# The second layer's norm taken in two halves, with the projection's blocks in another order

## The chip, the cores and the metric

One NeuronCore of one Trainium2 chip runs the whole program. The metric is the device time of one execution in microseconds; three runs of the kernel before gave 2537.19 to 2538.4, with a median of 2538.09.

## What is computed

Two blocks of a model follow one another. The change touches only the first, a two-layer block over 256 tokens of x and 256 tokens of context, model width 1024. Each layer norms its input, shifts and scales it by terms that differ for x and for the context, mixes, and adds the result. The second layer (the "odd" one) needs from its projection this:

```python
xl = rms_norm(h_lat, norm_w[li]) * (1.0 + scale_l[:, None, :]) + shift_l[:, None, :]
xc = rms_norm(h_ctx, norm_w[li]) * (1.0 + scale_c) + shift_c
cq_l, ckv_l, kr_l, z_l = jnp.split(xl @ w_in, ODD_SPLITS, axis=-1)   # 256, 128, 64, 1024 columns
cq_c, ckv_c, kr_c, z_c = jnp.split(xc @ w_in, ODD_SPLITS, axis=-1)
qn_l, qr_l = queries(cq_l, seq)          # rms_norm(cq, q_norm_w) @ wq_b
k_l, v_l = keys_values(ckv_l, kr_l_rot, seq)
k_c, v_c = keys_values(ckv_c, kr_c, clen)
out_l = (o_l.reshape(bsz, seq, C_WIDTH) * jax.nn.silu(z_l)) @ w_out
```

The query latent cq and the gate z are used for x alone. Only the key/value latent ckv (with its rotary part) is used for the context too.

## The kernel before

Every engine has its own program in each stage (an `nc.Block()`), and a stage starts when all engines have ended the one before it. Activations stand feature-major: the residual `k.h` is 128 partitions x 8 chunks x 512 tokens, tokens 0 to 255 of x and 256 to 511 of the context. A float32 product is made of three: operand and weight are split into a high and a low part (`xn_hi`/`xn_lo`, `w_hi`/`w_lo`), and hi*hi, hi*lo and lo*hi are summed in a PSUM bank.

Weights come in blocks of up to 256 columns through a ring of four slots, in the order of `k.plan`, filled by SyncE; a slot is free when its `w_lo` is made. `Split` cuts a block into four parts (`PARTS`), each two of the eight chunks deep. ScalarE copies a part to `w_hi` (L366), and GpSimd subtracts to get `w_lo` (L375); there are four buffers of each, so ScalarE waits for TensorE to have used the part four back (`consumed`).

The stages around the change:

- `project_out(..., "even")` ends the first layer. Beside it `EarlySquares` squares the new residual on ScalarE (L923), adds up six of the chunks' squares on VectorE, and TensorE, at its end, sums the rest over partitions with a matrix of ones into bank 7 (L910, L913), 512 tokens at a time.
- `odd_project` is the stage in question. `project` runs it: TensorE first does `norm.hum` warming products (`hum`, L270) that have no result, then blocks 0 to 5: cq (256 columns, 2 token groups of x), ckv (192 columns, 4 token groups, x and context), and four z blocks (256 columns, feature-major, x alone). Before each part of block 0 it waits for the two chunks of `xn` that the part needs.
- `RmsNorm` makes `xn` in it. VectorE scales the sum (`ask_root`, L255), ScalarE takes the root (L265, `root`), VectorE the reciprocal (L258), all 512 tokens wide. Then a pipeline goes over the eight chunks: VectorE `h * rstd` (L803), ScalarE shift and scale (L835, once for x and once for the context) and copy to `xn_hi` (L840), VectorE subtraction to `xn_lo` (L856).
- The program of ScalarE, VectorE and GpSimd in `project` is one loop over b from -1: first the `w_hi` and `w_lo` of block b+1, then (at b = -1) the norm, then the copies of block b out of its PSUM banks, then what `LatentNorms` has for this b. Each engine takes its instructions in this order.
- `LatentNorms` norms the latents. VectorE takes squares and sums (L1491, L1493), asks for the root (L1522, L1524), applies the rotary terms (L1060 to L1065, L1532), and scales (L1538). TensorE turns the latents (L1504, L1507) before block 4, and VectorE copies them out (L1544, L1546).
- `odd_queries` is the next stage; its first products (L1596) read the turned latents.

## Time and profile before

| | us |
|---|---|
| median of three runs | 2538.09 (2537.19 to 2538.4) |
| the profiled execution | 2540.84 |
| its span in the trace | 2539.1 |
| TensorE busy, of the span | 2404.1 |
| VectorE busy | 1640.1 |
| ScalarE busy | 1310.7 |
| GpSimd busy | 597.5 |

The stretch that the change touches is some 65 us near 360 to 423 of the span. All times in the rows are from the span's start. In a timeline a row "start, length" may merge several instructions of one form ("x4"); the brackets at its end tell how long its engine stood idle before it and which instruction ended that. Instructions of one engine overlap a little, so a row's start can lie before the end of the one above.

### The profile page before, as it was taken

The page shows a single profiled execution, that of the slowest core. Times are in us where ns is not written, and L with a number is a line of the kernel's source. Part 1 is how long each engine was busy: PE and PEld are TensorE (multiplying, and loading weights), DVE is VectorE, ACT ScalarE, POOL GpSimd, SP SyncE. Part 2 cuts the span into 40 slices and gives each one's busy share as a digit, 9 for nine tenths or more (in the row PEclk, how much of TensorE's full clock was granted, in tenths as well). Part 3 has the DMA queues.
Part 4 walks back from the last instruction along what each step waited for, and adds up shares of the span by engine and source line. Part 5 has one row for each costly group of instructions (what it writes and reads, how often), then busy time and mean ns, then how long its engine had stood idle before and what let it go on. Part 6 is the DMA issues. An engine that isn't in the chain of part 4 may idle for free. (4 is left out here: it accounts for less than half of the span.)

```text
span 2539.1 us, 61096 instructions
## 1 busy us (share of the span) xinstructions
PE 2404.1 (95%) x22840; PEld 2268.0 (89%) x22840; DVE 1640.1 (65%) x3412; ACT 1310.7 (52%) x2403; POOL 597.5 (24%) x484
## 2 busy tenths in 40 slices
PE   5999788999989999999999999879999999999998
PEld 3998567578978999999999999768999999999997
DVE  3032643535445967778888666665967778888666
ACT  3322643456346665555445554556666555445554
POOL 0335134158336930000000000636920000000000
PEclk8999999999999999999999999989999999999999
DMA  8554023043123555444444554324555444444552
GB/s 277 160 173 150 17 63 108 28 129 123 44 67 129 190 188 181 164 163 159 166 164 164 189 190 157 126 76 134 188 192 168 164 165 166 166 165 165 185 194 84
DMA packets 153875, 373.31 MB, mean 147 GB/s; under 512 B 8920, under 2 KB 102888, under 8 KB 137232
## 3 DMA queue, kind: packets, MB, share of 16 engines
q1 hardware_dynamic: 151232, 369.27, 43.3%
q10 hardware_dynamic: 2512, 2.24, 0.3%
q8 instruction: 88, 1.44, 0.2%
q14 instruction: 43, 0.35, 0.0%
HBM read 370.44 MB, written 1.05 MB: 146 GB/s over the span
## 5 line engine op out<-in xcount | busy, mean ns | idle before, releaser
L3027 ACT ACTIVATE w_hi<-ring 128x512 fp32r<-128x512 f32 x1024 | 641.8, 632 | 674.0 <-PE bank L3082 360.4
L3033 DVE TENSOR_TENSOR w_lo<-ring,w_hi 128x512 fp32r<-128x512 f32 x864 | 589.2, 690 | 330.5 <-ACT w_hi L3027 323.6
L3082 PE MATMUL bank<-hidden_hi,w_hi 128*128 128x256 f32 x2048 | 574.9, 281 | 1.4 <-ACT hidden_hi L3165 1.4
L3064 PE MATMUL bank<-x_hi,w_hi 128*128 128x256 f32 x2048 | 575.4, 281 | 0.2
L3082 PE MATMUL bank<-hidden_hi,w_lo 128*128 128x256 f32 x2048 | 573.1, 280 | 0.0
L3064 PE MATMUL bank<-x_hi,w_lo 128*128 128x256 f32 x2048 | 572.3, 279 | 0.0
L3064 PE MATMUL bank<-x_lo,w_hi 128*128 128x256 f32 x2048 | 571.0, 279 | 0.0
L3082 PE MATMUL bank<-hidden_lo,w_hi 128*128 128x256 f32 x2048 | 570.2, 278 | 0.0
L375 POOL TENSOR_TENSOR w_lo<-ring,w_hi 128x512 fp32r<-128x512 f32 (+3 forms) x260 | 338.6, 1321 | 663.5 <-ACT w_hi L366 655.0
L3082 PEld LDWEIGHTS bank<-hidden_hi,w_hi 128*128 128x128 f32 x2048 | 385.1, 188 | 1.6 <-issue 1.6
L3064 PEld LDWEIGHTS bank<-x_hi,w_hi 128*128 128x128 f32 x2048 | 385.0, 188 | 0.8 <-ACT w_hi L3027 0.6
L3082 PEld LDWEIGHTS bank<-hidden_lo,w_hi 128*128 128x128 f32 x2048 | 385.1, 188 | 0.0
L3064 PEld LDWEIGHTS bank<-x_lo,w_hi 128*128 128x128 f32 x2048 | 385.1, 188 | 0.0
L3064 PEld LDWEIGHTS bank<-x_hi,w_lo 128*128 128x128 f32 x2048 | 384.8, 188 | 0.0
L3082 PEld LDWEIGHTS bank<-hidden_hi,w_lo 128*128 128x128 f32 x2048 | 384.8, 188 | 0.0
L366 ACT ACTIVATE w_hi<-ring 128x512 fp32r<-128x512 f32 (+2 forms) x264 | 157.2, 614 | 285.2 <-PE bank L465 273.6
L3429 POOL MEMSET small<- 128x128 f32 x2 | 0.4, 207 | 949.6 <-DVE hidden L3324 949.6
L3033 POOL TENSOR_TENSOR w_lo<-ring,w_hi 128x512 fp32r<-128x512 f32 x160 | 203.3, 1301 | 33.5 <-ACT w_hi L3027 30.5
L465 PE MATMUL bank<-w_hi,xn_hi 128*128 128x256 f32 (+1 forms) x496 | 141.9, 286 | 4.5 <-DVE xn_lo L856 4.0
L465 PE MATMUL bank<-w_lo,xn_hi 128*128 128x256 f32 (+1 forms) x496 | 139.7, 282 | 0.0
L465 PE MATMUL bank<-w_hi,xn_lo 128*128 128x256 f32 (+1 forms) x496 | 139.4, 281 | 0.0
L3317 DVE TENSOR_TENSOR small<-small 128x1536 bf16<-128x1536 bf16 x128 | 121.8, 952 | 0.0
(518 smaller groups left out, 3966.5 us busy)
## 6 DMA issues: line engine op xcount, KB each, us to landing
ring<-in_peer_uT SPq DMA_DIRECT2D x128, 1024.0 KB, 4.9
ring<-in_peer_v SPq DMA_DIRECT2D x128, 1024.0 KB, 4.8
ring<-in_even_w_in SPq DMA_DIRECT2D x26, 1024.0 KB, 5.4
ring<-in_ada_w SPq DMA_DIRECT2D x24, 1024.0 KB, 7.8
ring<-in_odd_w_in SPq DMA_DIRECT2D x12, 1024.0 KB, 5.3
ring<-in_even_w_out SPq DMA_DIRECT2D x8, 1024.0 KB, 5.7
ring<-in_odd_w_out SPq DMA_DIRECT2D x8, 1024.0 KB, 5.2
ring<-in_peer_w_q SPq DMA_DIRECT2D x8, 1024.0 KB, 5.1
```

Source lines behind the costliest of these rows:

```text
L366: act.activation(k.hi[g % PARTS][:, 0:n], src, ACT.Copy).then_inc(k.hi_ready, 1)
L375: eng.tensor_tensor(k.lo[g % PARTS][:, 0:n], src, k.hi[g % PARTS][:, 0:n].bitcast(F32), ALU.subtract).then_inc(k.lo_ready, 1)
L465: mm = pe.matmul(out, lhs, rhs, start=(j == 0 and cc == 0 and q == 0), stop=(cc == KC - 1 and q == 2), skip_group_check=True)
L3027: act.activation(k.hi[q][:, :], k.ring[slot][:, q * PART:q * PART + PART], ACT.Copy).then_inc(k.hi_ready, 1)
L3033: eng.tensor_tensor(k.lo[q][:, :], k.ring[slot][:, q * PART:q * PART + PART], k.hi[q][:, :].bitcast(F32), ALU.subtract).then_inc(k.lo_read ...
L3064: mm = pe.matmul(k.bank[s][:, j * T:j * T + T], a[q][:, w], b[:, cc, :], start=(cc == 0 and n == 0), stop=(cc == KC - 1 and n == 2))
L3082: mm = pe.matmul(out, a[q][:, w], b[:, j, :], start=first and cc % 2 == 0 and n == 0, stop=last and cc % 2 == 1 and n == 2, skip_group_che ...
L3317: dve.tensor_tensor(right, spread(hot, 2, 3), spread(self.gateT[:, at, :, :], 3, HALF_J // 2), ALU.mult).then_inc(self.ready, 1)
L3429: pool.memset(self.k.ones, 1.0).then_inc(self.ones_ready, 1)
```

## The change

The norm of the second layer is taken by halves of 256 tokens: `early` is "halves". The sums go to two banks (7 for x, 6 for the context), the root of the first half is asked for and taken first, and on ScalarE it stands ahead of the `w_hi` copies of block 0. The chunk pipeline runs over the eight chunks of x; the second root follows; the pipeline over the context's chunks (`rest`) comes in the loop at b = 0, behind the `w_hi` and `w_lo` of block 1 and the copies of block 0. The blocks come in the order cq, z0, z1, ckv, z2, z3, so that the one that reads the context is the fourth, and the weights are planned in the same order. TensorE waits for the context's chunks at block 3. The steps of `LatentNorms` move along: the sums of cq to b = 1, those of ckv to b = 3, rotary and scaling to b = 4, the transposes behind block 5 and the copies to b = 5. The warming products of this stage are 12 in place of 48.

```diff
@@ project
+                    if norm and norm.halves and b == 3:
+                        norm.wait_chunk(pe, KC + KC // PARTS * (part + 1) - 1)
...
+                if norm and norm.halves and b == 0 and name != "pool":
+                    norm.rest(name, eng)
@@ RmsNorm
-        self.hum = {0: 8, 1: 48, None: 54}[layer]
+        self.hum = {0: 8, 1: 12, None: 54}[layer]
+        self.halves = early == "halves"
+        self.sums = [k.bank[7][:, 0:T], k.bank[6][:, 0:T]]
+    def ask_half(self, dve, half):
+        t = slice(half * T, half * T + T)
+        dve.wait_ge(self.summed, half + 1)
+        self.k.ask_root(dve, self.rstd[:, t], 1.0 / D, 1e-6, self.sums[half])
+    def scalar_half(self, act, half):
+        k = self.k
+        done = []
+        for i in range(KC * half, KC * half + KC + 1):
+            if i < KC * half + KC:
+                c, _, t = self.half_of(i)
+                act.wait_ge(self.scaled, i + 1)
+                o = self.work[:, c, t]
+                done.append(k.act.step(act.activation(o, o, ACT.Identity, bias=k.mod[:, self.layer, c, half:half + 1],
+                                                      scale=k.mod[:, self.layer, 8 + c, half:half + 1])))
+            if i > KC * half:
+                c, _, t = self.half_of(i - 1)
+                k.act.settle(act, done[c])
+                act.activation(self.out[0][:, c, t], self.work[:, c, t], ACT.Copy).then_inc(self.rounded, 1)
+    def vector_half(self, dve, half):
+        for i in range(KC * half, KC * half + KC + 2):
+            if i < KC * half + KC:
+                c, _, t = self.half_of(i)
+                dve.tensor_tensor(self.work[:, c, t], self.k.h[:, c, t], self.rstd[:, t], ALU.mult).then_inc(self.scaled, 1)
+            if i >= KC * half + 2:
+                c, _, t = self.half_of(i - 2)
+                dve.wait_ge(self.rounded, i - 1)
+                dve.tensor_tensor(self.out[1][:, c, t], self.work[:, c, t], self.out[0][:, c, t].bitcast(F32), ALU.subtract).then_inc(self.ready, 1)
+    def rest(self, name, eng):
+        (self.scalar_half if name == "act" else self.vector_half)(eng, 1)
     def squares(self, act):
-        pass
+        if self.halves:
+            self.root_half(act, 0)
     def scalar(self, act):
+        if self.halves:
+            self.scalar_half(act, 0)
+            self.root_half(act, 1)
+            return
     def vector(self, dve):
+        if self.halves:
+            self.ask_half(dve, 0)
+            self.vector_half(dve, 0)
+            self.ask_half(dve, 1)
+            return
@@ EarlySquares.tensor
+        if self.rms.halves:
+            halves = [(self.rms.sums[s], slice(s * T, s * T + T)) for s in range(2)]
+            for out, t in halves:
+                pe.matmul(out, k.ones[:, :], self.acc[:, t], start=True, stop=False)
+            pe.wait_ge(self.squared, KC)
+            for out, t in halves:
+                pe.matmul(out, k.ones[:, :], self.sq[:, 0, t], start=False, stop=False)
+                pe.matmul(out, k.ones[:, :], self.sq[:, 1, t], start=False, stop=True).then_inc(self.rms.summed, 1)
+            return
@@ odd_project
+    at = ["cq", 0, 1, "ckv", 2, 3]
+    width = {"cq": C_Q, "ckv": C_KV + C_R}
...
@@ LatentNorms
     def tensor(self, pe, b):
-        if b != 4:
+        if b != 6:
             return
         k = self.k
         pe.wait_ge(self.normed, 1)
-        pe.wait_ge(k.drained["dve"], self.counts[1]["dve"])
+        pe.wait_ge(k.drained["dve"], self.counts[3]["dve"])
+        pe.wait_ge(k.drained["act"], self.counts[4]["act"])
     def scalar(self, act, b):
-        if b == 2:
+        if b == 4:
             self.k.root(act, self.ss[:, :])
     def vector(self, dve, b):
-        if b == 0:
+        if b == 1:
...
-        if b == 1:
+        if b == 3:
...
+        if b == 4:
             for m in range(4):
...
-        if b == 2:
             dve.wait_ge(k.rooted, k.asked)
...
-        if b == 4:
+        if b == 5:
             dve.wait_ge(self.turned, 1)
@@ plan_weights
-    plan_columns(k, d["odd_w_in"], 0, C_Q)
-    plan_columns(k, d["odd_w_in"], C_Q, C_Q + C_KV + C_R)
-    plan_columns(k, d["odd_w_in"], C_Q + C_KV + C_R, C_Q + C_KV + C_R + D)
+    z = C_Q + C_KV + C_R
+    for c0, c1 in ((0, C_Q), (z, z + 2 * WB), (C_Q, z), (z + 2 * WB, z + D)):
+        plan_columns(k, d["odd_w_in"], c0, c1)
```

## Rows read from the trace of the kernel before

**Rows 1.** The page, busy time of each engine over the span.
```profile
PE 2404.1 (95%) x22840; PEld 2268.0 (89%) x22840; DVE 1640.1 (65%) x3412; ACT 1310.7 (52%) x2403; POOL 597.5 (24%) x484
```

**Rows 2.** Waits of TensorE, 350 to 425: total, times, longest.
```profile
PE bank L1504 <- DVE ckv L1538: 5.4, 1, 5.4
```

**Rows 3.** Timeline of TensorE, 355 to 423: start, length, instruction, idle before.
```profile
355.62 1.98 PE L913 MATMUL bank<-sq_even,ones 128*128 128x512 f32 x4 [1.60 <-ACT sq_even L923]
357.93 10.52 PE L270 MATMUL bank<-ident 128*128 128x512 bf16 x48 [0.32 <-PEq L419]
369.79 0.36 PE L465 MATMUL bank<-w_hi,xn_hi 128*128 128x256 f32 x1 [1.34 <-DVE xn_lo L856]
...
401.30 0.28 PE L465 MATMUL bank<-xn_hi,w_lo 128*128 128x256 f32 x1
407.00 1.08 PE L1504 MATMUL bank<-ident,cq 128*128 128x128 f32 x4 [5.42 <-DVE ckv L1538]
...
409.45 0.56 PE L465 MATMUL bank<-xn_hi,w_hi 128*128 128x256 f32 x1
...
422.93 3.69 PE L1596 MATMUL bank<-cqT,ring 128*128 128x256 f32 x16 [0.94 <-PEq L419]
```

**Rows 4.** Timeline of ScalarE, 354 to 377.
```profile
354.94 1.15 ACT L923 ACTIVATE sq_even<-residual 128x512 f32<-128x512 f32 x2 [10.08 <-DVE residual L1672]
357.96 2.19 ACT L366 ACTIVATE w_hi<-ring 128x512 fp32r<-128x512 f32 x4 [1.87 <-PEq L419]
360.06 0.61 ACT L265 ACTIVATE rms_rstd<-rms_rstd 128x512 f32<-128x512 f32 x1
364.82 2.08 ACT L835 ACTIVATE normed<-normed,mod 128x256 f32<-128x256 f32 x4 [4.15 <-DVE normed L803]
...
376.87 1.33 ACT L366 ACTIVATE w_hi<-ring 128x384 fp32r<-128x384 f32 x3
```

**Rows 5.** Timeline of VectorE, 360 to 412.
```profile
360.70 3.35 DVE L258 RECIPROCAL rms_rstd<-rms_rstd 128x512 f32<-128x512 f32 x1 [2.08 <-ACT rms_rstd L265]
...
379.62 0.76 DVE L520 COPY cq<-bank 128x256 f32<-128x256 f32 x2 [1.85 <-PE bank L465]
...
390.39 1.15 DVE L520 COPY ckv<-bank 128x192 f32<-128x192 f32 x4 [7.93 <-PE bank L465]
...
398.11 0.17 DVE L1524 TENSOR_SCALAR odd_ss<-odd_ss 128x4 f32<-128x4 f32 x1
...
400.79 2.89 DVE L1538 SCALAR_TENSOR_TENSOR cq<-cq,odd_ss,rows 128x256 f32<-128x256 f32 x2
403.60 3.14 DVE L1538 SCALAR_TENSOR_TENSOR ckv<-ckv,odd_ss,rows 128x128 f32<-128x128 f32 x4
...
410.44 1.28 DVE L1546 COPY ckvT<-bank 128x512 f32<-128x512 f32 x2
```

**Rows 6.** Timeline of GpSimd, 358 to 407.
```profile
358.67 4.96 POOL L375 TENSOR_TENSOR w_lo<-ring,w_hi 128x512 fp32r<-128x512 f32 x4 [14.64 <-ACT w_hi L366]
...
400.71 5.36 POOL L375 TENSOR_TENSOR w_lo<-ring,w_hi 128x512 fp32r<-128x512 f32 x4 [2.66 <-ACT w_hi L366]
```

**Rows 7.** Line 1538, the four ckv scalings: min/median/max ns, first and last start.
```profile
L1538 DVE SCALAR_TENSOR_TENSOR ckv<-ckv,odd_ss,rows x4: 338/842/1349, 403.6 to 406.4; 128x128 f32<-128x128 f32 x4
```

**Rows 8.** Timeline of VectorE in the final norm, 256 tokens wide.
```profile
531.81 1.75 DVE L258 RECIPROCAL rms_rstd<-rms_rstd 128x256 f32<-128x256 f32 x1 [2.92 <-ACT rms_rstd L265]
533.60 1.10 DVE L803 TENSOR_TENSOR normed<-residual,rms_rstd 128x256 f32<-128x256 f32 x3
...
540.24 0.76 DVE L856 TENSOR_TENSOR x_lo<-normed,x_hi 128x256 fp32r<-128x256 f32 x2 [0.52 <-ACT x_hi L840]
```

**Rows 9.** Timeline of ScalarE there.
```profile
531.36 0.42 ACT L265 ACTIVATE rms_rstd<-rms_rstd 128x256 f32<-128x256 f32 x1
```

**Rows 10.** Half-microsecond windows: length, busy of each engine, granted clock (PEclk), DMA.
```profile
404.50:405.00 0.50, 0.00 (x0) 0.00 (x0) 0.50 (x2) 0.00 (x0) 0.50 (x2) 0.64 0.00 0
...
411.00:411.50 0.50, 0.50 (x5) 0.50 (x3) 0.50 (x2) 0.00 (x0) 0.00 (x0) 0.53 0.00 0
```

More of the change, by code:

```diff
@@ L785, in sum, with half_of, root_half @@
             mm.then_inc(self.summed, 1)
+    def half_of(self, i):
+        half, c = divmod(i, KC)
+        return c, half, slice(half * T, half * T + T)
+    def ask_half(self, dve, half):
+        t = slice(half * T, half * T + T)
+        dve.wait_ge(self.summed, half + 1)
+        self.k.ask_root(dve, self.rstd[:, t], 1.0 / D, 1e-6, self.sums[half])
+    def root_half(self, act, half):
+        self.k.root(act, self.rstd[:, half * T:half * T + T])
+    def scalar_half(self, act, half):
[23 more added lines that the diff above has]
+        (self.scalar_half if name == "act" else self.vector_half)(eng, 1)
     def shift_chunk(self, act, c):
@@ L1457, in odd_project @@
 def odd_project(k, xn, cq, ckv, zT, norm, beside):
+    at = ["cq", 0, 1, "ckv", 2, 3]
+    width = {"cq": C_Q, "ckv": C_KV + C_R}
     def outs(b):
-        if b < 2:
-            return [("token", m) for m in range(2 if b == 0 else 4)]
+        if at[b] in width:
+            return [("token", m) for m in range(2 if at[b] == "cq" else 4)]
         return [("feature", [(0, P), (P, 2 * P)])]
     def store(name, eng, b, i, bank):
-        if b < 2:
-            dst = cq[:, i, :] if b == 0 else ckv[:, i, 0:C_KV + C_R]
+        if at[b] in width:
+            dst = cq[:, i, :] if at[b] == "cq" else ckv[:, i, 0:C_KV + C_R]
             return copy(name, eng, dst, bank[:, 0:dst.shape[1]])
-        return copy(name, eng, zT[:, 2 * (b - 2):2 * (b - 2) + 2, :], bank[:, :].rearrange("p (f t) -> p f t", f=2), ACT.Silu)
-    project(k, xn, T, [WB, C_KV + C_R] + [WB] * 4, outs, store, lambda b, i: "dve" if b < 2 else "act", norm=norm, beside=beside)
+        return copy(name, eng, zT[:, 2 * at[b]:2 * at[b] + 2, :], bank[:, :].rearrange("p (f t) -> p f t", f=2), ACT.Silu)
+    project(k, xn, T, [width.get(x, WB) for x in at], outs, store, lambda b, i: "dve" if at[b] in width else "act", norm=norm, beside=beside)
 class LatentNorms:
@@ L1515, in vector @@
         k, S = self.k, self.k.dve
-        if b == 0:
+        if b == 1:
             dve.wait_ge(k.drained["dve"], self.counts[0]["dve"])
             self.sums(dve, self.jobs()[0:2], 0)
-        if b == 1:
-            dve.wait_ge(k.drained["dve"], self.counts[1]["dve"])
+        if b == 3:
+            dve.wait_ge(k.drained["dve"], self.counts[3]["dve"])
             self.sums(dve, self.jobs()[2:6], 2)
@@ L1715, in first_block @@
             to_feature_major(k, jobs, "even_mix", True)
-            rms = RmsNorm(k, 1, TC, rstd, "sums")
+            rms = RmsNorm(k, 1, TC, rstd, "halves")
             project_out(k, mixT, TC, residual(0), "even", EarlySquares(k, rms, "even"))
@@ L1778, in __init__ @@
         self.hum = 24
+        self.halves = False
         k.norms += 1
```

## The prediction

> **What bounds the kernel now.** The page's first line comes first: TensorE is busy 2404 of 2539 us, so time is saved only where TensorE stands still or runs at a low clock [rows 1]. The reader then goes to the stretch that the diff touches, the projection of the second layer, from the end of the stage before it to the first product of the stage after it. TensorE's own timeline gives its borders [rows 3]: the sums of squares end at 357.60, the warming products run 357.93 to 368.45, the first product of the projection starts at 369.79, the transposes wait until 407.00, and the next stage starts at 422.93. Two holes stand in it. The first is 357.6 to 369.8, the norm. The second is 5.4 us before the transposes, which the list of waits puts on the scaling of the latents by VectorE [rows 2]. The ScalarE, VectorE and GpSimd timelines then tell what fills these holes [rows 4 to 6], and the granted clock tells what the second costs after it [rows 10]: TensorE stopped at 401.58, the grant fell to half at about 404.6 (3.1 us later), and came back at about 411.5, 4.5 us after work resumed at 407.0. TensorE loses half of such a stretch, about 2.2 us.
>
> **One fact that carries the sum.** While GpSimd has its subtraction w_lo running, a VectorE instruction with two SBUF tensors waits for it. The six latent scalings took 2.89 us for two and 3.14 us for four while GpSimd had four w_lo in a row [rows 5, 6]; one alone, after GpSimd was done, took 0.34 us against up to 1.35 [rows 7]. GpSimd's four took 5.36 us there and 4.96 us when VectorE was doing a one-tensor operation: 1.24 us each alone, and about 1.41 us for a pair of one w_lo and one VectorE operation.
>
> The page "Advanced Engine Details and Errata" of the Trainium skill, section "GPSIMD Details", says the Pool engine shares a read and a write interface with VectorE and conflicts with VectorE instructions of two SBUF inputs. That is the rule under the rows just named, and by it the third rival below could not happen; the rows alone already make it unlikely.
>
> **The change part by part,** on the clock of the trace of before.
>
> (a) The sums. The last two squares end at 356.09 [rows 4]. Now both halves wait for the second square, and eight 256-column records follow at about 0.21 us each, where 512-column ones took 0.43 and the first pair started at 355.62 [rows 3]. They end about 0.5 us later, near 358.1, and the next stage starts near 358.4: a loss of 0.5.
>
> (b) The first root. Its three steps at 256 columns: a scaling of 0.42 (the width of the three that took 1.10 together, starts 0.34 apart [rows 8]), the root 0.42 [rows 9], the reciprocal 1.75 [rows 8]. It now goes ahead of the four w_hi copies (2.19 us [rows 4]). It ends at 358.4 + 2.6 + about 0.1 = 361.1, where before it ended at 360.70 + 3.35 = 364.05 [rows 5].
>
> (c) The collision. Before, GpSimd's four w_lo were done at 363.63, ahead of the first scaling [rows 6]. Now w_hi begins at 359.2, w_lo at 359.9, and these go on to 365.4 beside VectorE's chunks. The first three scalings and the first x_lo each wait for one w_lo: they end at 361.5, 362.9, 364.3 and 365.7. The second x_lo follows at 366.4, and block 0's first product can start at 366.5: 3.3 us before 369.79, not the 5 or more that the halved norm alone would give.
>
> (d) Block 0. The warming is cut to 12 products, 12/48 of 10.52, so it ends at 361.2, and TensorE stands still for 5.3 us. I take it that the grant falls, as it did in the 5.4 us hole. Eight z parts took 390.39 to 401.58, so a part is 1.40 us and a block 5.6. From 366.5 the low level lasts to 371.0, with 2.24 us of full-rate work done. The remaining 3.4 end at 374.4, where before block 0 ended at 379.6 (VectorE starts on it at 379.62 [rows 5]). At full clock it would be bound by the chunks and end near 373. The lead is 5.2 us.
>
> (e) The second half. A first half pass takes 7.40 us from the first scaling to the last x_lo at this width in the final norm (533.60 to 541.00 [rows 8]); here ScalarE's shift costs about 0.50 a piece (four in 2.08 [rows 4]) against about 0.4 there, so I take 7.8. With the collision the first pass ends at 371.2. VectorE's second root takes 2.7, to 373.9, then the two copies of block 0 (0.76 [rows 5]) at 374.4, and only at 375.2 the second pass. Two w_lo of block 1 are still to come, so two scalings wait for them, another 2.0 us, and ScalarE issues its last x_hi copy at 384.5. Queued behind it on ScalarE are the w_hi copies of block 2 (the loop takes them after the norm's rest), and behind these GpSimd's w_lo: 0.63 + 1.3 + slack gives TensorE its block 2 at 386.6. Block 1 runs 374.4 to 380.1. So a new hole of 6.5 us opens between z blocks, where before there was none, and the clock falls in it too: 2.24 us lost after it. This hole is what eats the lead.
>
> (f) The rest of the blocks. Block 2: 386.6 + 5.6 + 2.24 = 394.5. Block 3, the context's, took 379.62 to 390.39: 10.7 to 10.8, so 405.2. Blocks 4 and 5: 11.3, so 416.5.
>
> (g) The latents. From the end of the ckv block to the root's request took 7.9 us (390.39 to 398.28 [rows 5]), with GpSimd's w_lo beside it, and so it will be: 413.2. Rotary terms and reciprocal take 2.5 us more (to 400.79). The six scalings cost 5.95 us before under w_lo; now block 5's last w_lo is over by 413, and they go at their own pace, at 0.26 to 0.34 each and slack: 2.0. So normed is at 417.7 and TensorE waits 1.2 us at the transposes in place of 5.4. At full clock the transposes take half of the 2.45 us between 407.00 and 409.45 [rows 3]. The copies out of PSUM now stand bare, where before block 4 covered them: from the transposes' end at 409.45 to 411.72 [rows 3, 5], 2.2 us. With 0.33 for the border of the stages (357.60 to 357.93) the next stage starts at 417.7 + 1.2 + 2.2 + 0.3 = 421.4, against 422.93. That is a gain of 1.5 to 1.6 us.
>
> (h) Weights. The same six blocks are loaded in another order; a slot comes free when its w_lo is done, so the fifth and sixth blocks are asked for at 365 and 378, over 20 us before use: nothing. The moved root of the latents and its table load on ScalarE stand before VectorE's request and cost nothing. If that cover went, the table load would be 1.3 us.
>
> The same sum by the skill's page "VectorE: DVE Perf Modes", section "The TRN2 errata": it asks for tiles of at least 512 elements, since each instruction pays a fixed part, and gives an fp32 tensor_tensor (N+151)/0.96 ns. By that, an estimate, 32 half-width operations cost 13.6 us where 16 full ones cost 11.0, so 2.6 us against the change. The trace agrees on single durations (0.42 here) but the operations overlap at 0.34 apart, so the sum above goes by these.
>
> **The sum.** -1.6 us. The profiled execution took 2540.84 us around a span of 2539.1, the median of the shown runs is 2538.09; the difference is applied to the median: 2536.5.
>
> **The rivals.**
> - Small holes (0.2). The grant doesn't fall before block 0, or comes back sooner, and the second pass misses one w_lo: up to 1.4 + 1.3 + 1.0 more. Together about 2533.5. For it: 5.3 us is near the length at which the rows show one fall. Against it: block 2 still waits for the whole second pass.
> - The clock at the end (0.2), the slower side. In the last 5 us TensorE works only 1.25 us, between a wait of 1.2 and one of 2.5. If the grant falls there, the transposes cost 1.2 more and the next stage's first 4.5 us lose 2.2; with a later return after the middle hole, 1.2 more. That is -1.6 + 4.6 = +3.0: 2541.1. [...]
> - No collision (0.05). If VectorE and GpSimd didn't exclude each other, block 0 starts at 364.4, block 2 at 381.6, and the next stage at about 415.5: 2531. Against it speak [rows 5 to 7].
> - The change doesn't do what it says (0.05). If block 0 starts no earlier than before, since the w_hi copies and w_lo hold the first half up, the 3.3 us of (c) are lost and the time is about 2539.8.
> - My forecast, with holes of 5 and 6.5 us and a gain of 0 to 3 us: 0.5.
>
> **The numbers.** Measurement can tell about 0.2%, 5.1 us, from no change. Only the third rival and the far end of the first pass that line below (0.08 together), and only the second with a further fall passes it above (0.05). Same: 0.87. The range takes in the first, second and fourth: 2532.5 to 2541.5.
>
> **What would show it.** In the new profile: the first product of block 0 near 366.5; VectorE's first scalings each ending just after a w_lo; a TensorE hole of about 6.5 us between blocks 1 and 2, put on w_hi or w_lo of block 2; the granted clock at 0.5 behind it; a wait of 1 to 2 us before the transposes and short latent scalings. The forecast is wrong if block 2 starts before 383, if the scalings are short while w_lo runs, or if the next stage starts at half clock.

## The result, and the profile after

The changed kernel took 2543.16 us (median of 20 runs) where the kernel before took 2539.11 (20 runs) in the same comparison: a ratio of 1.0016, 95% interval 1.001 to 1.0022. That is slower by about 4 us, outside the forecast range and on its other side. The span of the profiled execution was 2542.0 us.

The page, busy time of each engine: TensorE is busy as long as before [rows 1], so the page by itself says only that the time was lost where TensorE stood still, and not where that was. It executes 30 instructions less; remember the count.

```profile
PE 2403.7 (95%) x22810; PEld 2273.0 (89%) x22810; DVE 1643.6 (65%) x3430; ACT 1312.4 (52%) x2412; POOL 597.0 (23%) x484
```

**The changed stage is faster, as forecast.** TensorE's timeline after, which answers to [rows 3] (start, length, instruction, idle before). This execution reached the stage 1.28 us earlier (the last product of the residual ended at 351.88, before at 353.16):

```profile
357.18 2.75 PE L270 MATMUL bank<-ident 128*128 128x512 bf16 x12 [0.32 <-PEq L419]
365.33 0.55 PE L467 MATMUL bank<-w_hi,xn_hi 128*128 128x256 f32 x1 [5.41 <-DVE xn_lo L828]
...
385.50 0.55 PE L467 MATMUL bank<-xn_hi,w_hi 128*128 128x256 f32 x1 [5.90 <-ACT w_hi L366]
...
416.41 1.04 PE L1576 MATMUL bank<-ident,ckv 128*128 128x128 f32 x8
```

TensorE's waits from 355 to 421 (total, times, longest) answer to [rows 2]. The single wait of 5.4 us for the latents is gone; two of 5.4 and 5.9, one of 1.1 and one of 2.2 have come, and the wait for the last squares has grown from 1.6 [rows 3] to 2.1:

```profile
PE bank L467 <- ACT w_hi L366: 5.9, 1, 5.9
PE bank L467 <- DVE xn_lo L828: 5.4, 1, 5.4
PE bank L1665 <- PEq L419: 2.2, 1, 2.2
PE bank L972 <- ACT sq_even L988: 2.1, 1, 2.1
PE bank L1573 <- DVE ckv L1607: 1.1, 1, 1.1
```

VectorE's timeline, against [rows 5]: the first three scalings of the norm take 3.24 us beside GpSimd's w_lo, while the six latent scalings, now free of it, take 2.0 where they took 6.0.

```profile
359.87 3.24 DVE L824 TENSOR_TENSOR normed<-residual,rms_rstd 128x256 f32<-128x256 f32 x3
...
413.93 0.88 DVE L1607 SCALAR_TENSOR_TENSOR cq<-cq,odd_ss,rows 128x256 f32<-128x256 f32 x2
414.73 1.13 DVE L1607 SCALAR_TENSOR_TENSOR ckv<-ckv,odd_ss,rows 128x128 f32<-128x128 f32 x4
```

The windows below give length, busy time of TensorE, weight loads, VectorE, ScalarE and GpSimd, then granted clock, DMA share and GB/s. TensorE's clock is at its lower level, 1.2 GHz (0.50), behind each of the two long holes, and at 2.4 GHz (1.00) in the rest of the stage.

```profile
364.50:371.50 7.00, 6.17 (x29) 6.20 (x30) 5.45 (x15) 5.70 (x14) 0.06 (x1) 0.51 0.49 150
371.50:381.50 10.00, 8.10 (x69) 7.89 (x67) 7.48 (x15) 6.71 (x15) 5.16 (x4) 1.00 0.35 105
382.00:388.00 6.00, 2.50 (x12) 2.53 (x13) 3.44 (x8) 5.33 (x10) 4.00 (x4) 0.50 0.00 0
```

From the last product of the residual to the next stage's first product the stage takes 67.81 us; before it took 69.77 [rows 3]. So 2.0 us were gained here, and by the medians some 6 lost elsewhere; between the two profiled executions, whose spans differ by 2.9 us, it is 4.9.

**Where they were lost.** ScalarE's table loads are good landmarks: each execution has the same 92, in the same order. From one to the next, the two traces agree within their usual scatter but for one place, 130 us behind the changed stage, in the second block's recurrent projection. First before, then after (ScalarE's timeline):

```profile
550.87 1.28 ACT L1932 ACT_TABLE_LOAD   x1
553.92 1.28 ACT L1933 ACT_TABLE_LOAD   x1
575.86 1.28 ACT L1945 ACT_TABLE_LOAD   x1
```

```profile
547.57 1.28 ACT L2002 ACT_TABLE_LOAD   x1
552.28 1.28 ACT L2003 ACT_TABLE_LOAD   x1
576.82 1.28 ACT L2015 ACT_TABLE_LOAD   x1
```

I call the two stretches A and B. They took 3.05 and 21.94 us before, 4.71 and 24.54 after: 4.3 us lost, in code that the change doesn't touch. VectorE's timeline shows how A grew, first before, then after:

```profile
548.55 0.17 DVE L2003 TENSOR_TENSOR rk_heads<-cpart,cols 128x8 f32<-128x8 f32 x1 [0.28 <-DMA mu_lora<-in_mu_lora]
548.75 0.42 DVE L2007 TENSOR_TENSOR gkoT<-ktT 64x255 f32<-64x255 f32 x1
549.26 1.33 DVE L2009 SCALAR_TENSOR_TENSOR ktT<-gkoT,mu_lora,ktT 64x256 f32<-64x256 f32 x1
```

```profile
545.70 1.18 DVE L2073 TENSOR_TENSOR rk_heads<-cpart,cols 128x8 f32<-128x8 f32 x1 [0.71 <-DMA mu_lora<-in_mu_lora]
```

GpSimd's row of four w_lo in the same stretch, first before, then after (GpSimd's timeline):

```profile
548.84 5.76 POOL L375 TENSOR_TENSOR w_lo<-ring,w_hi 128x512 fp32r<-128x512 f32 x4 [0.84 <-ACT w_hi L366]
```

```profile
545.56 5.39 POOL L375 TENSOR_TENSOR w_lo<-ring,w_hi 128x512 fp32r<-128x512 f32 x4 [0.85 <-ACT w_hi L366]
```

VectorE waits 0.71 us for the load mu_lora, before 0.28. Before, rk_heads and the first gkoT started ahead of GpSimd's row, gkoT by 0.09 us, and took 0.17 and 0.42 us. After, rk_heads starts 0.14 us behind the start of the row and waits for a w_lo: 1.18 us for an operation of 0.17, and nearly every two-tensor operation behind it waits for one as well. It is the collision of step (c), at another place. TensorE, which before never waited more than 0.3 us here, then has a hole ahead of its products of L1972, and in B the granted clock falls; before it was 1.00 throughout. TensorE's timeline and the windows from 550 us on, after:

```profile
554.14 4.18 PE L1972 MATMUL bank<-ktT,wa 32*128 32x256 f32 x16 [1.30 <-ACT ktT L2003]
```

```profile
550.00:555.00 5.00, 3.70 (x29) 3.44 (x28) 2.10 (x4) 3.12 (x6) 1.37 (x2) 1.00 0.95 301
555.00:560.00 5.00, 5.00 (x22) 3.94 (x21) 0.00 (x0) 5.00 (x15) 4.53 (x4) 0.57 0.12 36
560.00:565.00 5.00, 5.00 (x35) 5.00 (x35) 0.00 (x0) 1.91 (x5) 2.23 (x2) 0.75 0.70 210
```

And the load comes late by one DMA issue in SyncE's train of 11 small loads. SyncE's timeline before, then after:

```profile
542.96 0.43 SPq L511 DMA_DIRECT2D masks<-in_mask  x1
543.43 0.43 SPq L511 DMA_DIRECT2D gla_w<-in_gla_a_w  x1
```

```profile
539.67 0.43 SPq L515 DMA_DIRECT2D masks<-in_mask  x1
540.14 1.44 SPq L515 DMA_DIRECT2D gla_w<-in_gla_a_w  x1
```

The same issue takes 0.43 and 1.44 us. What lengthens it was found only with the later runs: the list of DMA queues for one microsecond shows a 16 KB transfer of queue q8, kind "instruction". It lies in the window 534 to 535 before, 6.6 us ahead of the train, and in 540 to 541 after, on the very issue. First before, then after (packets, MB, share of the window):

```profile
q8 instruction: 1, 0.02, 8.2%
```

```profile
q8 instruction: 1, 0.02, 6.5%
```

### The profile page after: what moved, and what is told of

It reads as the page before. It is cut to its first block and busy times, and to the rows that moved or that the text cites. A ratio compares the mean times of both kernels' runs of the same rounds, so it can differ in the third digit from the quotient of the medians.

```text
span 2542.0 us, 61064 instructions
## 1 busy us (share of the span) xinstructions
PE 2403.7 (95%) x22810; PEld 2273.0 (89%) x22810; DVE 1643.6 (65%) x3430; ACT 1312.4 (52%) x2412; POOL 597.0 (23%) x484
## 5 line engine op out<-in xcount | busy, mean ns | idle before, releaser
L366 ACT ACTIVATE w_hi<-ring 128x512 fp32r<-128x512 f32 (+3 forms) x264 | 157.1, 613 | 278.3 <-PE bank L467 268.8
```

The costliest lines, as they stand in the source:

```text
L366: act.activation(k.hi[g % PARTS][:, 0:n], src, ACT.Copy).then_inc(k.hi_ready, 1)
```

## The experiments

"Stage" is the time from the residual's last product to the next stage's first; "next part" is from there to ScalarE's next table load. Ratios are to runs of the kernel before in the same comparison. Each expectation was fixed before its run.

### Is it there again?

e1 is the kernel before, e2 the changed one, with no edit.

> The kernel before, unchanged, to see how far the stages of one kernel scatter between two traces. Theory A (the loss of the changed kernel sits behind the changed stage, in the lower-rank projection of the second block near 545 to 577 us, and is fixed): this trace has the same lengths as the first one there, the issue of gla_w takes 0.43 us, the load of mu_lora lands before GpSimd's first w_lo, and the stretch from the table load near 551 to the one near 576 takes 25.0 us again. Theory B (that stretch varies from execution to execution, and both kernels have it): the stretch differs by more than 1 us between the two traces of the same kernel. Time ratio 1.000 by both, within 0.0007.

> The changed kernel, unchanged. Theory A: from the end of the stage before the norm to the first product of the next stage it takes 67.8 us again, against 69.8 before, a gain of 2.0; and the issue of gla_w again takes 1.4 us in place of 0.43, the stretch from the table load near 548 to the one near 577 takes 29.2 us again against 25.0; ratio near 1.0016. Theory B: the changed stage takes 67.8 again, but the stretch behind comes out between 25 and 29 and the issue times differ from the first trace; then the 4 us of the median must be looked for in a mean of many places.

Measured: e1 2538.3 us, ratio 1.0000 (0.9991 to 1.0009); e2 2540.78, 1.0015 (1.0006 to 1.0024). Stage 69.29 and 67.55, so a gain of 1.7 here. A and B: 2.87 and 22.00 in e1, 4.68 and 21.37 in e2, where the clock did not fall in B. But e2 showed a second loss, in the next part: 30.18 us for 28.50. Its window right behind the next stage's start:

```profile
421.50:424.50 3.00, 3.00 (x7) 2.44 (x8) 0.00 (x0) 0.00 (x0) 0.00 (x0) 0.50 0.03 8
```

This is the second rival of the prediction, the clock at the end. Of the nine changed kernels without an edit there (the first profile, e2 to e4, e6 to e9, e16) four show it, and none of the five of the kernel before.

### The stage: are the two holes what the prediction takes them for?

**e3.** The w_hi copies of block 2 no longer wait for the whole second half; one goes behind every second copy of it.

```diff
-                    if h < PARTS * n and act:
+                    if h < PARTS * n and act and not (norm and norm.halves and b == 1):
...
+                if high and c % 2 == 1:
+                    high(c // 2)
```

> The changed kernel with ScalarE's four w_hi copies of block 2 taken in among the context's chunks of the norm (one after every second chunk) in place of behind them. If the 5.9 us hole between blocks 1 and 2 is due to these copies standing behind the norm's rest on ScalarE, as the prediction's step (e) has it, block 2 follows block 1 with a hole under 1 us, no fall of the clock comes after it, and the stage from the end of the residual to the next stage's first product takes 60 to 61.5 us in place of 67.8: 6.5 to 8 us less than the changed kernel, so about 3 us less than the kernel before (ratio 0.9985). If the hole is due to VectorE (its two-tensor operations waiting for GpSimd), only 2 to 3 us are won, since the woven w_lo delay the chunks further and block 3 then waits for them.

Measured: 2538.35 us, ratio 1.0002 (0.9993 to 1.0011), stage 65.2. The waits say what the hole of 5.9 turned into:

```profile
PE bank L467 <- DVE xn_lo L830: 5.4, 1, 5.4
PE bank L467 <- POOL w_lo L375: 3.5, 4, 1.4
```

The single hole behind ScalarE's queue is gone, as step (e) would have it, and the clock stays at 1.00 behind it. But only 2.4 us of the stage come back (65.2 for 67.55 in e2), where the expectation asked for 6.5 to 8 if the queue were all of it: TensorE now waits four times for a w_lo. That is the 2 to 3 us that the expectation gave for a hole due to VectorE and GpSimd, so the queue was the last of several waits and not the only one. A and B were 4.69 and 24.61.

**e4.** 36 warming products in place of 12 (`1: 36` for `1: 12` in `self.hum`).

> The changed kernel with 36 warming products in place of 12. If the low clock in block 0 is due to the 5.4 us hole behind the 12 products: the grant stays at full, block 0 is bound by the chunks, ends 1.0 to 1.5 us earlier, and the stage takes 66.3 to 66.8 us in place of 67.8; ratio to before about 1.0011. If the cost of the low clock in block 0 is hidden by what VectorE and ScalarE do meanwhile (second root, w_hi of block 1), the stage gains under 0.4 us.

Measured: 2539.98 us, ratio 1.0009 (1.0000 to 1.0018), stage 67.41. The clock stays up in block 0, but the stage is only 0.1 to 0.4 us shorter than in e2 and in the first trace: block 2 starts no earlier, since it waits for w_hi (5.9 us as before). Next part 30.12.

**e7.** As e3, with the w_hi behind the copies 0, 1, 2 and 4.

> As the woven kernel, but the w_hi copies of block 2 stand behind the shifts of the context's chunks 0, 1, 2 and 4, not behind the copies of chunks 1, 3, 5 and 7. In the woven kernel the hole of 5.9 us was replaced by four waits of 3.5 us in sum for w_lo, and the stage took 65.2 us. If these waits come from the late places in ScalarE's order, they go, block 2 follows block 1, and the stage takes 60 to 61.5 us, with a ratio to the kernel before near 0.9985 (the fixed 1.7 us behind the stage still in it). If they come from the exclusion of GpSimd and VectorE, the waits move to block 3's chunks and the stage takes 63.5 to 65.

Measured: 2544.33 us, ratio 1.0007 (0.9998 to 1.0016), stage 68.4. Neither branch of the expectation came out. Block 2 now follows with a wait of 0.7 us, but the hole stands ahead of block 3 and is ended by that block's own w_hi: on ScalarE it is queued behind the second half, whose last copy ends 1.7 us later than in e3 (388.05 for 386.40), a table load of 1.28 us and a copy of block 1. The hole moved and shrank only from 5.9 to 4.5 us.

```profile
PE bank L467 <- ACT w_hi L366: 4.5, 1, 4.5
```

**e8.** GpSimd waits for the whole first half before it makes the w_lo of block 0.

```diff
+                if norm and norm.halves and b == -1 and low:
+                    norm.wait_chunk(eng, KC - 1)
```

> The changed kernel, where GpSimd waits with the w_lo of block 0 until the first half of the norm is done, so that none runs beside VectorE's first chunks. If the exclusion made the three first scalings take 3.24 us and the first x_lo 1.48, they now take 1.1 and 0.42, the first half of the norm is done about 2.3 us earlier (near 12.7 us after the norm's root is asked for in place of 15), and TensorE's first product waits for w_lo instead, starting 1 to 2 us later than in the changed kernel. If the scalings are slow for another reason (the reads of the residual, ScalarE's copies beside them), they stay at 3.2 us.

Measured: 2545.61 us in its one run, which allows no ratio; stage 71.11. VectorE's first three scalings, with no w_lo beside them:

```profile
359.72 1.09 DVE L826 TENSOR_TENSOR normed<-residual,rms_rstd 128x256 f32<-128x256 f32 x3
```

1.09 us against 3.24: the collision costs 0.72 us for each of them, which settles step (c). Paying for it by a late w_lo is worse, though: TensorE waits 9.2 us for the first and starts 3.8 us later than in the change, where I had expected 1 to 2.

### The place 130 us later

**e5.** The kernel before, with two more loads, of 0.69 us together, ahead of the train.

```diff
+                scratch = k.sb("scratch", [8, 512])
+                recurrent_project(k, b, [(scratch[:, 0:256], c("headrow")[0:8, 0:256]), (scratch[:, 256:512], c("headrow")[0:8, 256:512]),
...
```

> The kernel before with two small loads more (of data it has, into a tile that nobody reads) ahead of the eleven loads of the second block's recurrent projection, so that these are issued about 0.8 to 1 us later. Theory A (the changed kernel loses behind its own stage since a late last load makes VectorE's first two-tensor operation miss the time before GpSimd's first w_lo): the stretch between the two table loads near 551 and 554 takes 4.7 us in place of 2.9 to 3.1, in the kernel that otherwise has nothing of the change, and the time is 1.7 us longer, or up to 4.9 in executions where the grant falls there (ratio 1.0005 to 1.0018). Theory B (the 1.7 us are no matter of these loads): the stretch stays at 3.0 and the ratio at 1.000.

Measured: 2544.17 us, ratio 1.0008 (0.9999 to 1.0017). A and B: 4.69 and 24.60. VectorE:

```profile
549.24 1.14 DVE L2003 TENSOR_TENSOR rk_heads<-cpart,cols 128x8 f32<-128x8 f32 x1 [0.76 <-DMA mu_lora<-in_mu_lora]
```

So both parts of the loss, in A and in B, appear in the trace of the kernel before, without the change, as soon as its loads are late by this much. The ratio agrees with a loss of 3.2 us (0.0013), but its interval reaches to no loss as well.

**e6.** The changed kernel; ScalarE's queue issues the last six loads.

```diff
+            if act and len(loads) > 8:
+                for dst, src in loads[5:]:
+                    eng.dma_start(dst, src).then_inc(loaded, 16)
...
-            for dst, src in loads:
+            for dst, src in (loads[:5] if len(loads) > 8 else loads):
```

> The changed kernel, where ScalarE issues the last six of those eleven loads and SyncE the first five, so that all land 2 us or more earlier. Theory A: the stretch between the table loads is back at 2.9 to 3.1 us, no fall of the grant near 555, and of the changed kernel's loss 1.7 us and the share of the falls go: ratio to the kernel before 1.000 to 1.0006 in place of 1.0015. Theory B: the stretch stays at 4.7 and the ratio at 1.0015.

Measured: 2543.55 us, ratio 1.0010 (1.0001 to 1.0019), A 4.84. The cure failed: VectorE waited longer for the load than before, not less. SyncE now issued the next weights at 543.75, while ScalarE was at its issues for mu_lora, and that these got ahead of it is a likely reason but was not tested.

```profile
550.90 0.82 DVE L2076 TENSOR_TENSOR rk_heads<-cpart,cols 128x8 f32<-128x8 f32 x1 [2.30 <-DMA mu_lora<-in_mu_lora]
```

**e9 and e10.** rk_heads moved behind its six neighbours, in the changed kernel and in the kernel before.

```diff
-            do(dve.tensor_tensor(b["rsel"][:, :, :], spread(b["headsel"], 1, 4), spread(k.col("r_k", 0, 4), 2, 2), ALU.mult))
...
             self.nshifted = 2
+            do(dve.tensor_tensor(b["rsel"][:, :, :], spread(b["headsel"], 1, 4), spread(k.col("r_k", 0, 4), 2, 2), ALU.mult))
```

> The changed kernel with one instruction moved: in the second block's recurrent projection VectorE's two-tensor product rk_heads, which needs the late load mu_lora, stands behind the six small operations that follow it (its result is used only much later). Theory A (an operation that comes over 1 us late misses the gap before GpSimd's first w_lo and costs one w_lo more; the longer hole of TensorE then lets the granted clock fall in most executions): the stretch between ScalarE's two table loads near 551 and 555 us falls from 4.7 to 2.8-3.4 us, the next stretch to the load near 579 is 21.4-22.0 us and not 24.6, and the ratio to the kernel before is 0.9990-1.0003, against 1.0007-1.0016 of the change as it is. Theory B (the lateness itself, not the operation's place, sets the hole): the two stretches stay at 4.7 and 24.6 and the ratio stays above 1.0006.

> The kernel before with the same instruction moved, a control. Theory A: the instruction cost next to nothing there, since it came ahead of GpSimd's first w_lo: stretch between the loads near 551 and 555 us 2.7-3.1 (2.9-3.05 without the move), the next 21.4-22.0, ratio 0.9995-1.0003. If the ratio falls by as much as in the changed kernel with the move (0.9988 or less), the move is worth something by itself and says nothing of the change.

Measured: e9 2541.36 us, ratio 1.0014 (1.0004 to 1.0023), A 4.29, B 21.42; e10 2540.5, 1.0005 (0.9994 to 1.0016), A 2.86. The move bought 0.4 us of the 1.7, since now gkoT, which stands behind the same wait for the loads, is the first to come too late. It is the lateness and not this operation. In e10, the control, the move changed nothing (B 21.93).

**e11.** 16 warming products on TensorE behind the transposes.

```diff
         mm.then_inc(self.turned, 1)
+        k.hum(pe, k.bank[0], 16)
```

> The changed kernel with 16 warming products (as before a norm, some 1.7 us at full clock) on TensorE behind the transposes, in the 2.2 us in which it waits for VectorE's bare copies. Theory A (the clock falls in the next stage in over half of the executions because TensorE is nearly idle from 413 to 422 us, and costs 1.65 us then): the next stage's first part, from its first product to its table load, takes 28.5 us in the profile, granted clock 1.0 throughout; the next stage starts no later than without (67.6-67.9 us behind the last product of the residual); the median falls by 0.5-1.3 us: ratio to before 1.0004-1.0010. Theory B (the fall has its cause elsewhere): 30.1 us in over half of the executions as before and ratio unchanged, 1.0010-1.0016.

Measured: 2542.2 us, ratio 1.0014 (1.0004 to 1.0023), next part 28.5, stage 70.21. The clock stayed up, but I had sized the products wrongly. One takes 0.22 us and not 0.11 (48 in 10.52 [rows 3]), so 16 are not over when the copies are, and the next stage starts 1.5 us late. The other 0.9 of the stage's growth lay at its start, where the clock had already fallen behind the 2.12 us wait for the last squares (0.50 from 358 to 360 us); of the changed kernels only e6 shows this too. In e12 the same 16:

```profile
416.14 3.62 PE L270 MATMUL bank<-ident 128*128 128x512 bf16 x16
```

**e12.** e3, e4, e9 and e11 together.

> Four edits to the changed kernel at once: the w_hi of the third weight block taken between the copies of the second half of the norm, 36 warming products, rk_heads moved behind its neighbours, and the 16 warming products behind the transposes. Expected if each does what it did or is expected to do alone: stage from the last residual product to the next stage's first product 64.5-65.3 us (before 69.3-69.8), next part 28.5, the stretches near 551 to 579 together 24.5-25.2 as in the kernel before; sum 4.3-5.0 us under the kernel before, ratio 0.9980-0.9985. The rival: gains ahead are given back behind, as in the change itself (the loads near 545 land late, clock falls near 555): ratio 0.9990-1.0005.

Measured: 2537.82 us, ratio 0.9997 (0.9988 to 1.0006), stage 66.11, next part 28.5, A 2.87, B 22.00. The next part, A and B are as expected, the stage is 0.8 us longer than expected, and the ratio missed by far: by these stretches the kernel should be 3.7 us faster than before, and the ratio gives 0.8 (3.0 faster to 1.5 slower). This is not explained. Here no issue was long, although it is a changed kernel. That, and its 40 TensorE instructions more than the changed kernel, led to the last series.

### What moves the instruction transfer

Theory: q8 carries TensorE's instruction stream, and the number of TensorE instructions ahead sets at which point of the program the next 16 KB are fetched. The traces of before and after have 88 and 87 such transfers in the whole span.

**e14 and e16, the minimal pair.** One number each in `self.hum`: the kernel before with 12 warming products, the changed kernel with 48.

```diff
 e14
-        self.hum = {0: 8, 1: 48, None: 54}[layer]
+        self.hum = {0: 8, 1: 12, None: 54}[layer]
 e16
-        self.hum = {0: 8, 1: 12, None: 54}[layer]
+        self.hum = {0: 8, 1: 48, None: 54}[layer]
```

> The kernel before with 12 warming products in place of 48, nothing else. Theory A: the instruction transfer moves into the train of loads (1.2 to 2.5 us behind its start), one issue takes 1.2-2.0 us in place of 0.43-0.83, the stretch between the table loads near 551 and 555 us is 4.3-4.7 us (2.9-3.05 before), the sum to 579 us 25.7-26.1 or 29.3 (24.9 before). In the stage itself block 0 runs at half clock for some us: 0-1.5 us more. Ratio 1.0005-1.0020. Theory B: no long issue, 2.9-3.05 and 24.9; ratio 1.0000-1.0006.

> The changed kernel with the 48 warming products of the kernel before in place of 12, nothing else; the minimal pair to e14. They end 10.3 us after their start, some 2.5 us behind the arrival of the first operands, so the stage takes 69.5-70.5 us in place of 67.8. Theory A: instruction transfer ahead of the train, no long issue, 2.9-3.1 and together 24.8-25.0. Ratio 1.0000-1.0008, no worse than the change itself although the stage has lost all its gain. Theory B: long issue, 4.7, 25.7-29.3; ratio 1.0012-1.0022.

Measured: e14 2540.92 us, ratio 1.0004 (0.9994 to 1.0013); e16 2537.5, 0.9996 (0.9985 to 1.0006). The ratio of e14 is just under what I expected and would not settle it alone. That of e16 says more: with 36 more warming products and a stage of the same length (67.98 for 67.81) the changed kernel goes from 1.0016 and 1.0015 to 0.9996. The traces show the rest. SyncE in e14, and its transfer, in the window 542 to 543:

```profile
542.07 0.43 SPq L511 DMA_DIRECT2D masks<-in_mask  x1
542.54 1.34 SPq L511 DMA_DIRECT2D gla_w<-in_gla_a_w  x1
```

```profile
q8 instruction: 1, 0.02, 6.0%
```

In e16 the transfer is back in 530 to 531, 7.7 us ahead of the train, and the issue is short:

```profile
540.12 0.43 SPq L515 DMA_DIRECT2D gla_w<-in_gla_a_w  x1
```

A and B: 4.69 and 21.42 in e14, 3.05 and 21.93 in e16. Over all 19 profiled executions (of 17 kernels, two of them twice) the page's count of TensorE instructions sorts them without an exception. With 22804 to 22834 (e14; the changed kernel and e2, e3, e6 to e9 with 22810; e11 with 22826; e4 with 22834) the transfer falls 1.3 to 2.5 us behind the train's start. With 22840 to 22850 (the kernel before, e1, e5, e10; e17 with 22842; e13, e15, e16 with 22846; e12) it falls 6.0 to 8.7 us ahead of it. The issue right behind the transfer is long, 1.2 to 1.8 us for 0.42 to 0.43, in nine of the ten of the first kind; in the tenth, e6, ScalarE issued at that time, and there its pair for mu_lora took 2.37 us. It is long in none of the second kind. In all nine of these the transfer starts when TensorE has begun 3287 to 3290 of its products, although they come at different times; in the others it is 3292 to 3322. A transfer does not lengthen every issue, though: outside this train it began on 67 issues of SyncE in the 19 traces, and 62 of them took no longer than 0.45 us; the five longer ones are one and the same issue near 31 us. So it takes the transfer and the train together, and why is not known.

e16 missed my expectation for the stage by 2 us, to the good: 67.98 where I had said 69.5 to 70.5. Its first product came at 367.43 in place of 365.33, and the stage was hardly longer. Block 0 then runs at full clock, and block 2 starts at the same time as in the change (33.66 and 33.62 us behind the residual), so all that block 0 gains by an earlier start is taken by the hole ahead of block 2.

**e13 and e15.** 36 warming products more at places where TensorE waits anyway: 24 ahead of the norm, 8 behind the transposes, 4 ahead of the second block's projection (58 for 54). e13 is the changed kernel with them, e15 is e3 with them.

```diff
+        self.hum = {0: 8, 1: 36, None: 58}[layer]
...
+        k.hum(pe, k.bank[0], 8)
```

> The changed kernel with 36 TensorE instructions more, all warming products (0.213 us each) in places where it waits anyway: 36 and not 12 ahead of the norm, 8 behind the transposes, 4 more ahead of the second block's projection. Theory A (where a block of TensorE's instruction stream is fetched sets which SyncE issue takes 1 us longer): the 16 KB instruction transfer lands 5 to 9 us ahead of SyncE's train of 11 loads, no issue in it is long (gla_w 0.43 us), the stretch between the table loads near 551 and 555 us is 2.9-3.1 us and the two together to 579 us are 24.8-25.0; the stage stays at 67.4-67.9, the next one's first part at 28.5; ratio to before 0.9987-0.9996. Theory B (something else in the changed program): long issue, 4.7, and 25.7-29.3 as in the change; ratio 1.0002-1.0012.

> The changed kernel with the w_hi of the third weight block woven into the second half of the norm, and the same 36 TensorE instructions more as in e13 (without the moved rk_heads; e12 had 16 warming products at the end, which took 3.4 us and delayed the next stage by 1.5). Expected: stage 64.4-65.0 us, next part 28.5, stretches near 551 to 579 together 24.8-25.0: 4.8-5.3 us less than the kernel before by these, ratio 0.9978-0.9985. The rival is that e12's missing gain (0.5 us measured of the 3.7 that its first half was shorter) comes from elsewhere: then 0.9992-1.0000.

Measured: e13 2539.04 us, ratio 0.9999 (0.9990 to 1.0008), stage 67.4, next part 28.5; e15 2534.62, 0.9982 (0.9973 to 0.9991), stage 64.6, next part 28.5. No issue was long, as expected. But A was 4.29 and 4.69, B 24.46 and 24.53: this half of the expectation missed. The ratio of e13 is above the expected range, though its interval reaches into it; that of e15 is as expected, although its profiled execution lost 4.3 us in A and B. A profile shows one execution, and a ratio many. In e13 mu_lora was waited for 0.38 us in place of 0.28, and gkoT just missed the gap:

```profile
546.13 0.17 DVE L2074 TENSOR_TENSOR rk_heads<-cpart,cols 128x8 f32<-128x8 f32 x1 [0.38 <-DMA mu_lora<-in_mu_lora]
546.33 1.55 DVE L2078 TENSOR_TENSOR gkoT<-ktT 64x255 f32<-64x255 f32 x1
```

So the margin is about 0.1 us.

**e17.** e15 without the four products ahead of the second block's projection.

> e15 without the 4 warming products more ahead of the second block's projection (54 again), so 32 TensorE instructions more than the changed kernel. Theory A (the four delayed that projection's first product by 0.1 us against SyncE's loads or VectorE's work, and so VectorE's first two-tensor operation missed the gap ahead of GpSimd's first w_lo): instruction transfer 5-9 us ahead of the train of loads, DMA wait of VectorE 0.3 us, the stretches 2.9-3.1 and 21.9-22.0, together 24.8-25.0; ratio to before 0.9970-0.9980. Theory B (the loads land late by themselves in some executions, mu_lora landing 0.1 to 0.6 us later without a long issue): DMA wait over 0.35 us, 4.3-4.7, together 25.7-29.3, ratio 0.9978-0.9986. If 32 instructions are not enough, one issue is long as in the change.

Measured: 2535.01 us, ratio 0.9983 (0.9971 to 0.9994), stage 64.6, A 4.70, B 24.55. Without the four products the gap was missed as well, so they were not the cause, and it is theory B that came out:

```profile
542.76 1.14 DVE L2079 TENSOR_TENSOR rk_heads<-cpart,cols 128x8 f32<-128x8 f32 x1 [0.74 <-DMA mu_lora<-in_mu_lora]
```

The DMA records say what is left. Counted from the train's first issue, the last packet of mu_lora lands after 7.18 to 7.98 us in the executions with the long issue (e6 aside, and e5, whose two added loads bring it to 7.21), and the gap was missed in all of them. Without it it lands after 6.42 to 7.07; the gap was caught in five (6.42, 6.47, 6.52, 6.71, 6.71) and missed in e13, e17 and e15 (6.69, 6.91, 7.07). The landing has a scatter of its own that reaches over the edge of the gap; why these three were late stays open.

e15 and e17 beat both kernels. Of four edits to the changed kernel (the woven w_hi, the warming ahead of the norm, the 8 products at the end, the count of TensorE instructions) the first carries most of the stage: 2.4 to 2.9 us. By the ratios, the other three bring the change from 1.0015 to 0.9999 (e13), and the first from there to 0.9982 (e15).

## Why the prediction was wrong

Point by point, each time taken from the residual's last product (353.16 before, 351.88 after):

| step | forecast | measured | before |
|---|---|---|---|
| (a) warming starts | 5.2 | 5.30 | 4.77 |
| (b) first reciprocal ends | 7.94 | 7.96 | 10.89 |
| (c) block 0 starts | 13.3 | 13.45 | 16.63 |
| (d) VectorE takes block 0 | 21.2 | 22.19 | 26.46 |
| (e) block 2 starts | 33.4 | 33.62 | |
| (g) transposes | 64.5 | 64.04 | 53.84 |
| (g) next stage | 68.2 | 67.81 | 69.77 |

Every step inside the stage held within 1 us, and the gain was 2.0 us for 1.6 (1.7 between e1 and e2; the four traces of the kernel before with 48 warming products lie from 69.29 to 70.00). (d) is late since the low clock lasted 5.9 us behind the start of block 0, to 371.2, where the forecast took 4.5; the hole ahead of block 2 is shorter than forecast, 5.9 us for 6.5, so the two misses partly cancel in (e). The page "Advanced Engine Details and Errata" of the Trainium skill, section "GPSIMD Details", names the conflict of VectorE and GpSimd that stands behind (c); the trace agrees: without w_lo beside them each of the first three scalings was 0.72 us shorter (e8).

The step that failed is the last one, "the difference is applied to the median". It assumes that nothing behind the stage moves: of what stands behind, the sum has no term at all, and (h) looked only at the weights. Two things moved.

1. **The next stage's start at the lower clock,** my second rival, at 0.2. It came in four of nine, and where it came it cost 1.65 us and not 4.6. About 0.7 us on the mean. Its direction was right; chance and price were wrong, and the holes behind which it came were of 1.1 and 2.2 us, as forecast.
2. **The second block's projection,** which I had not looked at. Of the executions with A over 4 us, the clock fell in B in nine (24.5 to 24.6 us) and stayed up in five (21.4), so a missed gap gives A and B some 28.1 us for 24.9: about 3.2 lost. The chain: (d) takes 36 warming products away; a 16 KB instruction transfer moves into a train of loads; an issue takes 1 us longer; VectorE misses the gap ahead of GpSimd; a hole opens in TensorE; the clock falls in some executions. The count is shown by e14 and e16, the way from lateness to loss by e5, the collision by e8. That the transfer is what lengthens the issue rests on the two coming together in all 19 traces; why it should is not shown.

The terms sum to -2.0 + 0.7 + 3.2 = +1.9 us. The measured +4.05 (2.5 to 5.6 by its interval) lies above it, and so does e2 by its ratio, +3.8 (1.5 to 6.1). e16, which has neither term in its profile, should stand at -1.8 and by its ratio stands at -1.0 (-3.8 to +1.5). So the terms give the sign and about half of the size; the missing 2 us are not explained. One candidate: the stretch from the table load near 810 us to the one near 917 took 107.9 us in six of the fourteen executions of changed kernels and 106.88 in all others, all of it in a product's mean distance of 117.8 ns in place of 116.7, at a granted clock of 1. Other stretches have such steps in both kernels.

The forecast that the result would lie within 0.2% held; its sign did not. As a step it was the range that was too narrow: it took in what could happen in the stage and at its end, and nothing for the 2100 us behind it.

## What to carry to other kernels

A change of 2 us in one stage can be paid back twice in a stage that it doesn't touch. Look, in the trace of before, for near ties behind the change: a gap that an operation makes by 0.1 us, a hole behind which the clock may fall. Here they decided more than the sum did.

Warming products are instructions as well. Where their number is changed, compare the places of the instruction transfers with the trains of small loads, and where it matters, fill the count up again at a place where TensorE waits. In e16 this alone took the loss away.

An engine's queue that runs ahead with one half of the work is of little use while another's copies for the next block wait behind the second half: e16 gave up 2 us of head start and lost nothing by it, and e3 won 2.4 of the stage by reordering a queue alone.

## What the runs showed of the hardware

- Where an instruction transfer of 16 KB fell into this train of DMA issues, one issue took 0.8 to 1.4 us longer (ten of ten executions, nine on SyncE and one on ScalarE, against none of nine where it came 6.0 to 8.7 us ahead). Issues outside the train were not lengthened by one (62 of 67).
- A two-tensor VectorE operation beside a row of w_lo on GpSimd mostly takes 0.8 to 1.5 us, and its size hardly matters: 0.17 became 1.18 for 128x8, 0.42 became 1.48 for 128x256.
- TensorE's clock fell or stayed up in executions of one and the same kernel behind the same holes: behind two waits of 1.1 and 2.2 us at the stage's end (four of nine), and behind a wait of 1.3 us at the start of B (it fell in seven of ten; behind one of 0.8 in one of three, and behind one of 1.5 in e6).
